# Where two engines leave a pass of experts: VectorE's branch behind twelve of sixteen pairs, TensorE's with its sides exchanged, in a two-block transformer kernel

## The reference

```python
def hier_moe(x, rg_w, rg_b, re_w, re_b, w_gate, w_up, w_down):
    ...
    g_star = jnp.argmax(lg, -1)                       # one of 4 groups for each row
    ...
    top_v, top_i = lax.top_k(le, TOP_K_IN_GROUP)      # 2 of its 8 experts
    ...
    for g in range(N_GROUPS):
        h = jax.nn.silu(jnp.einsum('td,edf->tef', t, w_gate[g])) * jnp.einsum('td,edf->tef', t, w_up[g])
        y = y + jnp.einsum('tef,efd->td', h * gate[:, g, :, None], w_down[g])
    return y.reshape(B, S, D)

def second_block(x, ...):
    for l in range(DEPTH):
        mix = hybrid_mixer(x, ...)
        x = layer_norm(DEEPNORM_ALPHA * x + mix, ln1_g[l], ln1_b[l])
        moe = hier_moe(x, ...)
        x = layer_norm(DEEPNORM_ALPHA * x + moe, ln2_g[l], ln2_b[l])
    return x
```

## Time and profile before

| | us |
|---|---|
| median of 3 runs | 1676.3 (1675.8 to 1680.1) |
| profiled execution, device time | 1679.1 |
| its span | 1677.4 |
| TensorE busy | 1645.6 (98%) |
| VectorE busy | 856.5 (51%) |
| ScalarE busy | 651.1 (39%) |
| GpSimd busy | 172.1 (10%) |

### The profile page before, as it was taken

The page is one execution under the profiler, slowest core; times in us unless marked ns, Lnnn a source line. Parts: engine busy times, 40 slices in busy tenths (PEclk is TensorE's granted clock), DMA queues, the critical chain, the costliest instruction groups (busy, mean ns, idle before and its releaser), DMA issues. The chain is left out here.

```text
span 1677.4 us, 23534 instructions
## 1 busy us (share of the span) xinstructions
PE 1645.6 (98%) x9403; PEld 1244.0 (74%) x9403; DVE 856.5 (51%) x1420; ACT 651.1 (39%) x920; POOL 172.1 (10%) x242
## 2 busy tenths in 40 slices
PE   9999999999999999999999999999999999999997
PEld 7888879999798887999988975444448887544442
DVE  6566564444646556544456867322126785532223
ACT  5455444343445454434345453111114464211111
POOL 2020001111202000111111040000002023000000
PEclk9999999999999999999999999999999999999999
DMA  8544545553654455455356546999995636699996
GB/s 319 180 146 147 179 151 183 194 178 123 235 184 134 151 176 176 167 185 188 137 185 194 189 142 231 408 421 421 421 397 191 192 127 241 228 421 420 421 417 259
DMA packets 158587, 396.61 MB, mean 236 GB/s; under 512 B 20752, under 2 KB 85264, under 8 KB 140048
## 3 DMA queue, kind: packets, MB, share of 16 engines
q1 hardware_dynamic: 158480, 395.18, 64.6%
HBM read 394.10 MB, written 1.05 MB: 236 GB/s over the span
## 5 line engine op out<-in xcount | busy, mean ns | idle before, releaser
L946 PE MATMUL ps<-split,split 128*128 128x256 f32 (+3 forms) x1872 | 631.6, 337 | 1.2 <-DVE split L939 0.7
L950 PE MATMUL ps<-split,split 128*128 128x256 f32 (+3 forms) x1872 | 627.6, 335 | 0.1
L947 PE MATMUL ps<-split,split 128*128 128x256 f32 (+3 forms) x1872 | 623.6, 333 | 0.0
L924 DVE TENSOR_TENSOR split<-ring,split 128x2048 fp32r<-128x2048 f32 x136 | 312.5, 2305 | 253.9 <-ACT split L917 253.8
L946 PEld LDWEIGHTS ps<-split,split 128*128 128x128 f32 x1872 | 351.6, 188 | 36.1 <-issue 2.1
L950 PEld LDWEIGHTS ps<-split,split 128*128 128x128 f32 x1872 | 351.7, 188 | 35.8 <-DVE split L2389 1.2
L947 PEld LDWEIGHTS ps<-split,split 128*128 128x128 f32 x1872 | 352.9, 189 | 33.0 <-issue 0.5
L917 ACT ACTIVATE split<-ring 128x2048 fp32r<-128x2048 f32 x136 | 260.3, 1916 | 278.1 <-PE ps L950 268.7
L1860 PE MATMUL ps<-ring,arena 128*64 128x512 f32 x464 | 105.7, 592 | 0.0
L3040 DVE SCALAR_TENSOR_TENSOR arena<-arena,ps 128x256 f32<-128x256 f32 x32 | 15.4, 480 | 169.8 <-ACT arena L2306 134.1
L1860 PE MATMUL ps<-arena 128*64 128x512 f32 x288 | 99.5, 594 | 0.5 <-SPq L1208 0.5
(11 more groups left out here) (260 smaller groups left out, 1698.8 us busy)
## 6 DMA issues: line engine op xcount, KB each, us to landing
ring<-in_w_in SPq DMA_DIRECT2D x52, 1024.0 KB, 5.1
ring<-in_w_gate_up SPq DMA_DIRECT2D x44, 1024.0 KB, 5.3
ring<-in_expert_w_down SPq DMA_DIRECT2D x32, 1024.0 KB, 13.0
ring<-in_w_down SPq DMA_DIRECT2D x22, 1024.0 KB, 4.9
ring<-in_w_in SPq DMA_DIRECT2D x28, 768.0 KB, 4.5
ring<-in_expert_w_gate SPq DMA_DIRECT2D x20, 1024.0 KB, 11.8
ring<-in_expert_w_up SPq DMA_DIRECT2D x20, 1024.0 KB, 13.8
arena<-in_expert_w_down SPq DMA_DIRECT2D x16, 1024.0 KB, 14.5
```

The lines of the kernel that those rows point to most:

```text
L924: nc.vector.tensor_tensor(split(slot), slot, split(high[:, n % HIGH, :]), ALU.subtract).then_inc(low_done.sem, 1)
L946: nc.tensor.matmul(acc, sh, mh, start=start, stop=False)
L947: nc.tensor.matmul(acc, *second, start=False, stop=False)
L950: return nc.tensor.matmul(acc, *third, start=False, stop=stop)
```

## The change

Three engines are changed; what is computed stays as it is.

- VectorE: `moe_pass` takes a first and a last pair. The first 12 pairs (`KNOWN_DUOS`) run ahead of the branch, and pairs 12 to 15 stand in both of its sides. The sides are exchanged: the one with a further pass comes first, the one that ends the layer is `Else`.
- TensorE: the branch stays behind the last scatter, with its sides exchanged. The fillers stand ahead of it, 18 instead of 14; `skip_pass` is what is left in `Else`.
- ScalarE: `leave_high2("xT", 0, l + 1)` moves into the branch, behind the three weight units.
- The first projections of TensorE are put into a function, called at the same place.

```diff
+KNOWN_DUOS = 12
...
                 def more_passes(done):
 
-                    with pe.If(passes <= done):
-                        skip_pass(PASSES - done)
-                        if l < LAYERS - 1:
-                            keep_running(bank2(("yg", 0, 0, 0)), 14)
-                    with pe.Else():
+                    if l < LAYERS - 1:
+                        keep_running(bank2(("yg", 0, 0, 0)), 18)
+                    with pe.If(passes > done):
                         moe_pass(done)
                         if done + 1 < PASSES:
                             more_passes(done + 1)
+                    with pe.Else():
+                        skip_pass(PASSES - done)
...
                 if l == 0:
                     high_parts2(0, 2, l)
-                leave_high2("xT", 0, l)
+                    leave_high2("xT", 0, l)
                 high_parts2(3, 3, l)
...
                     if l < LAYERS - 1:
                         high_parts2(0, 2, l + 1)
+                        leave_high2("xT", 0, l + 1)
...
-                def moe_pass(pass_):
+                def moe_pass(pass_, first=0, last=DUOS):
...
-                    for d in range(DUOS):
+                    for d in range(first, last):
...
-                passes = moe_pass(0)
+                passes = moe_pass(0, 0, KNOWN_DUOS)
 
                 def more_passes(done):
 
-                    with dve.If(passes <= done):
+                    with dve.If(passes > done):
+                        moe_pass(done - 1, KNOWN_DUOS)
+                        add_scattered(done - 1, False)
+                        moe_pass(done, 0, KNOWN_DUOS)
+                        if done + 1 < PASSES:
+                            more_passes(done + 1)
+                        else:
+                            moe_pass(done, KNOWN_DUOS)
+                            add_scattered(done, True)
+                            second_norm()
+                    with dve.Else():
+                        moe_pass(done - 1, KNOWN_DUOS)
                         add_scattered(done - 1, True)
                         second_norm()
                         skip_pass(PASSES - done)
-                    with dve.Else():
-                        add_scattered(done - 1, False)
-                        moe_pass(done)
-                        if done + 1 < PASSES:
-                            more_passes(done + 1)
-                        else:
-                            add_scattered(done, True)
-                            second_norm()
```

More of the change, by code:

```diff
@@ L1704, in _, with project_rows @@
             keep_running(bank_of(("gu", 2 * PAIRS - 1)), 26)
-            for l in range(LAYERS):
+            def project_rows(l):
                 turn_stream(l)
@@ L1708, in _ @@
                 project2("A", l)
+            for l in range(LAYERS):
+                project_rows(l)
                 project2("B", l)
@@ L3016, in turned_picks @@
                         last.then_inc(pT_in.sem, 1)
-                    if pass_ > 0:
+                    if first == 0 and pass_ > 0:
                         nc.vector.tensor_scalar(rank_flat, rank_flat, -float(TAKEN_SLOTS), None,
@@ L3021, in moe_pass @@
                         make_picks(0, pass_)
[L3022 to L3027, removed]
+                    if first == 0:
+                        for f in (1, 3):
+                            gathered(0, f)
+                        turned_picks(0)
+                        for four in range(1, FOURS):
+                            make_picks(four, pass_)
+                    if first == 0 and pass_ == 0:
                         for n in range(PASSES - 1):
```

## The result

The changed kernel takes 1680.4 us, the median of 19 runs (1678.1 to 1683.6), against 1677.6 us of 19 runs of the kernel before beside them (1675.5 to 1680.7). The ratio is 1.0016, 95% interval [1.0009, 1.0022]: 2.8 us slower, 1.5 to 3.7. That is within 0.3%, but it is neither the 1.6 us less that were forecast nor inside the range that ended at 1679.0.

The account below looks back on a forecast made before the run. TensorE, busy 98% of the 1677.4 us span, was taken as the bound, so only its holes or the tail could be won. Exit -1.7, TensorE's jump +0.1, the rest 0: -1.6 us, from 1676.3 to 1674.7 us; range 1671.8 to 1679.0.

Parts of the forecast that it names:

- Exit: End of layer 1: VectorE's far jump no longer delays the exit, SyncE's 1.9 us wait becomes 0.2; -1.7 us.
- VectorE, pair 12 (the cover): Jump of 5.5 to 6.2 us between pairs' L3052 and L3040, hidden by 7.9 us of room, 8.6 with weights; cost 0.
- Rival (c): Pair 12: the jump outlasts its cover, making the kernel slower; 1675.5 to 1682.9 us, say 1679; chance 0.12.
- VectorE's stall in layer 0: Before L2658 after the layer change: 6.2 us stall shrinks to under 1, but TensorE is late next; cost 0.
- TensorE's boundary: Layer change: L1568's start moves by -1.0 to +1.1 us, depending on how many queued matmuls fit; middle taken, +0.1.
- ScalarE, cost 0: Layer 0: its far jump, 3.3 us, loses its cover and L933 starts near 1275.0, but TensorE needs the result later.
- The sum: Whole kernel: -1.7 (exit) + 0.1 (TensorE's jump) + three zeros = -1.6 us, giving 1674.7 us.

Follow-up runs that it names:

- the first four pieces: Kernel before plus four unread one-piece 8 KB loads behind each of pairs 11 and 12 in each layer (first four meant): 1678.9 us, ratio 1.0006.
- twelve: Kernel before plus twelve unread one-piece 8 KB loads in each layer, behind ScalarE's last eviction of pair 10: 1681.6 us against 1678.0, ratio 1.0024.

## Why the prediction was wrong

- **Exit, -1.7 us: right.** 1.9 became 0.2 in every kernel with VectorE's part; with the jump behind the stream of weights it is worth 1.7 to 1.8 us by the medians.
- **VectorE, pair 12 (the cover): right on the engine, wrong as a cost.** The jump takes 5.1 to 5.7 us where it is bare (5.5 to 6.2 were taken), and VectorE's idle stayed at 5.95. The step that failed is "I cost it at 0". It counted VectorE's time and the room before TensorE's next need of it. It did not count what the jump asks of the transfer engines: two fetches of 8 KB, each of which sets one engine back by 0.97 us. In both layers that made it the last, by 1.50 and 2.0 us, and TensorE meets it at pair 13. I had even read the two facts that make it matter, that the stretch is full and that TensorE already waits at pair 13 for exactly these weights, and had used that wait as room ("8.6 with the weights"). It is the opposite of room: where TensorE already waits for a transfer, whatever delays its last share is paid in full. The term is +3.0 us of waits, and in layer 1 another 1.7 by the clock in the profiled execution.
- **Rival (c), the sign right and the mechanism wrong.** It had the kernel slower through pair 12, but by a jump that outlasts its cover; VectorE's idle ahead of that product shows that it did not. It was also the only case slower than the kernel before, with 0.12, and the range left out its far half, so it ended too low.
- **VectorE's stall in layer 0 goes, cost 0: right.** 6.23 became 0.79 us. In the kernel without VectorE's part the stall is back (6.24 us), and the time doesn't differ from that of before.
- **TensorE's boundary, +0.1: right within noise.** -0.2 us in the profile, no difference in the time of these parts alone. The clock differs there from execution to execution: from 1256 to 1275 us it was 0.82 before, 0.91 after, 0.82 with TensorE's and ScalarE's parts alone and 1.00 with the branch after fifteen pairs. In the changed kernel's execution it was 0.75 over 1263.8 to 1270.5 in place of 0.50, and layer 1's first product comes at 1444.26 for 1445.69. So the changed kernel's execution was lucky there and unlucky at pair 13 of layer 1, and the profiled spans came out equal by that.
- **ScalarE, cost 0: right.** Its L934 begins at 1273.63, not near 1275.0, behind 2.37 us of idle that TensorE's L951 ended, so its jump took less than the 3.3 us that I gave it; it cost nothing.
- **The sum.** With the term that was missing: -1.7 + 3.0 = +1.3 us, and 1.7 more where the clock falls behind one of the two holes, as it did in the profiled execution, +3.0. Measured: +2.8 (1.5 to 3.7). How often the clock falls over many executions isn't shown; holes of 2.07, 2.08, 2.51 and 2.83 us were followed by a fall, those of 1.95, 2.03 and 2.11 were not.

What stays open is why an instruction fetch of 8 KB takes 0.97 us from its engine when a load of 8 KB takes 0.31, while both packets last about 0.32 us. Open too is which engine a fetch goes to. In the layers followed here (both of the changed kernel, of VectorE's part alone and of the branch after nine) it was the last or up to 0.6 us ahead of it; whether it must be so near, these runs don't tell. No run has a fetch on an engine with 2 us to spare. That one would cost nothing is argued from the loads and from the lead of 0.45 and 0.62 us that the waits show as saved.

## What to carry to other kernels

A jump over much code is covered only if two things are: the time of the engine that jumps, and the transfers by which it loads its instructions. Here it did no harm behind the last transfers that someone waits for; so put it there, or where the transfer engines have a pause. Read a wait for a transfer, however short, as the sign that the next delay of its last share will be paid in full. When the sides of a branch are exchanged, what stood ahead of the jump may come to stand behind it, so a branch "left where it was" can be a different branch.

## What the runs showed of the hardware

- The 16 transfer engines run the same stream with a fixed stagger: the first share of a 1 MB transfer lands 1.8 to 2.9 us before the last. It differs from run to run and holds for tens of us. Work on a single engine is therefore free up to that engine's lead and costs 1:1 beyond it (the first four pieces: 0 us; twelve: a gap of 1.87 us).
- A lag in a full stream isn't made good: 2.1 us were still 2.07 us after 42 us. The Trainium skill, "DMA: Bandwidth & Descriptors", Why a DMA increments its semaphore by 16 and not by 1, says that the engines of one DMA finish independently and that only the full count means that all has landed; the waits here agree (2.51 us for one share of 16 that was 2.0 us late).
- Loads of 8 KB in one piece entered at one for every 0.92 us between the weights' packets, and each took 0.31 us from its engine. The same page, Queues, rings and completion order, has an engine take packets of its queues in turn, which goes with this spacing.
- The Trainium skill, "Runtime: NRT & Kernel Launch", Instruction fetch mechanics, has a taken branch whose target isn't loaded wait for its own fetch; VectorE's idle of 5.05 us agrees. The fetches also delayed the transfers of others, and here that was the part that cost time (+3.0 us of waits, with VectorE's own idle unchanged at 5.95).
